# The attention norm's root moved from the query product's input to the attention scores

## What is computed

```python
def rms_norm(x, g):
    y = x * rsqrt(mean(x * x, axis=-1) + EPS)
    return y * g

x1 = x + merged @ w_out                       # end of the mixing layer

def cross_attention(x1, k, v, g, wq, wo):
    h = rms_norm(x1, g)
    q = (h @ wq).reshape(B, S, XA_HEADS, XA_HEAD_DIM)
    s = einsum('bshd,bmhd->bhsm', q, k) * (XA_HEAD_DIM ** -0.5)
    p = softmax(s, axis=-1)
    o = einsum('bhsm,bmhd->bshd', p, v)
    return o @ wo
```

## Time and profile before

| | us |
|---|---|
| median of 3 runs | 1138.18 |
| lowest, highest | 1137.84, 1140.97 |
| the profiled execution's own time | 1140.06 |
| its span in the trace | 1138.3 |

### The profile page before, as it was taken

How to read it: one execution, slowest core, us unless ns; L and a number is a source line. 1 busy time by engine, 2 the same in 40 slices (tenths; PEclk the granted TensorE clock), 3 DMA queues, 4 the chain that set the end, 5 groups by cost and what they waited for, 6 DMA issues and landing times.

```text
span 1138.3 us, 18382 instructions
## 1 busy us (share of the span) xinstructions
PE 1077.6 (95%) x5851; PEld 793.5 (70%) x5851; DVE 815.3 (72%) x1616; ACT 630.9 (55%) x932; POOL 231.7 (20%) x197
## 2 busy tenths in 40 slices
PE   6999999899799999999999999999999999999991
PEld 5998459899449977666666666666666666666660
DVE  4734724454862355579999999999999888999993
ACT  4384333233633351566666666666667665667663
POOL 1002220001000020232222233322223332323331
PEclk7999999999999999999999999999999999999996
DMA  9502415250826181899999999999999999999945
GB/s 304 208 1 81 150 77 223 83 219 16 340 104 233 64 346 48 231 320 361 354 368 366 370 364 369 365 357 359 367 371 363 364 358 362 365 365 357 349 133 168
DMA packets 63558, 301.70 MB, mean 265 GB/s; under 512 B 13175, under 2 KB 15843, under 8 KB 36886
## 3 DMA queue, kind: packets, MB, share of 16 engines
q1 hardware_dynamic: 47038, 261.93, 60.0%
q0 software_dynamic: 16480, 39.24, 14.5%
HBM read 282.65 MB, written 36.17 MB: 280 GB/s over the span
## 4 chain that ended last, share of the span: by engine, by line
PE 86%; DMA 6%; DVE 4%; ACT 2%; issue 1%; SPq 1%; DVEq 0%; POOLq 0%; ACTq 0%
PE pair L179 17%; PE pair L1950 15%; PE pair L1975 15%; PE pair L1941 10%; PE pair L1957 7%; PE pair L1717 5%; PE pair L1928 5%; PE pair L1621 3%; DMA regB<-in_exp_w_down 2%; PE pair L1833 2%; PE pair L1901 1%; DVE regL L1154 1%; DMA regB<-in_cache_mem_k 1%; PE pair L1964 1%; DMA regA<-in_w_in 1%; PE pS L1913 1%
## 5 line engine op out<-in xcount | busy, mean ns | idle before, releaser
L758 POOL DMA_INDIRECT acc_rows<-regL x64 | 123.3, 1926 | 423.0 <-DMA acc_rows<-regL 245.5
L1975 PE MATMUL pair<-hi_parts,act_parts 128*96 128x512 f32 x512 | 163.2, 400 | 1.2 <-DVE act_parts L1559 1.2
L179 PE MATMUL pair<-h_hi,w_parts 128*128 128x260 f32 x640 | 132.2, 288 | 3.7 <-DVE h_lo L1148 3.4
L1950 PE MATMUL pair<-hi_parts,x_parts 128*96 128x512 f32 x512 | 132.4, 401 | 0.0
L179 PEld LDWEIGHTS pair<-h_hi,w_parts 128*128 128x128 f32 x640 | 105.1, 192 | 4.8 <-issue 2.8
L1975 PEld LDWEIGHTS pair<-hi_parts,act_parts 128*96 128x96 f32 x512 | 79.6, 165 | 28.2 <-DVE act_parts L1559 1.3
L1950 PEld LDWEIGHTS pair<-hi_parts,x_parts 128*96 128x96 f32 x512 | 79.8, 165 | 27.8 <-issue 1.9
L742 POOL DMA_INDIRECT regL<-h_rows,regL x67 | 68.7, 1025 | 58.7 <-DVE regL L1405 28.9
L1555 DVE TENSOR_TENSOR regB_lo<-regB,hi_parts 128x2048 fp32r<-128x2048 f32 x32 | 73.1, 2284 | 10.4 <-ACT hi_parts L1062 10.4
L1555 DVE TENSOR_TENSOR regA_lo<-regA,hi_parts 128x2048 fp32r<-128x2048 f32 x32 | 73.1, 2285 | 9.3 <-ACT hi_parts L1062 9.1
L1565 DVE TENSOR_SCALAR regL<-pair,regL 96x512 f32<-96x512 f32 x64 | 47.7, 746 | 40.7 <-PE pair L1975 40.7
(11 more groups left out here) (357 smaller groups left out, 2350.0 us busy)
## 6 DMA issues: line engine op xcount, KB each, us to landing
regA<-in_exp_w_gate SPq DMA_DIRECT2D x32, 1024.0 KB, 9.5
regA<-in_exp_w_up SPq DMA_DIRECT2D x32, 1024.0 KB, 17.0
regA<-in_exp_w_down SPq DMA_DIRECT2D x32, 1024.0 KB
regB<-in_exp_w_down SPq DMA_DIRECT2D x32, 1024.0 KB, 19.3
regB<-in_exp_w_gate SPq DMA_DIRECT2D x16, 1024.0 KB, 9.4
regB<-in_exp_w_up SPq DMA_DIRECT2D x16, 1024.0 KB, 18.3
regC<-in_exp_w_gate SPq DMA_DIRECT2D x16, 1024.0 KB, 9.0
regC<-in_exp_w_up SPq DMA_DIRECT2D x16, 1024.0 KB, 19.7
```

The lines of the kernel that those rows point to most:

```text
L179: ins = pe.matmul(pair[p][:, h, 0:HALF], w, x[:, k, cols], start=k == 0 and i == 0, stop=k == KD - 1 and i == 2)
L758: pool.indirect_dma_start(acc_rows, bass.IndirectOffsetOnAxis(ap=sidx[0:SLOTS, r:r + 1].bitcast(U32), axis=0), yX[r][0:SLOTS, :], None, bo ...
L1950: pe.matmul(gu_out, x_parts[:, x, k, :], hi, start=False, stop=False, skip_group_check=True)
L1975: ins = pe.matmul(pair[2][0:SLOTS, h, :], act_parts[:, x, k, :], w[:, k, h * 512:(h + 1) * 512], start=k == 0 and s == 0, stop=k == KF - 1 ...
```

## The change

The norm is split. ACT now makes the query product's high part straight from x1 and the norm's weight (`x_hi2` = rounded `xT` x `g`), and DVE makes its low part in one operation (`xT` x `g` - `x_hi2`, into `h2_lo`); both are made slab by slab during x1. The spreading of `rs`, the norm's multiplication and the tile `htmp2` fall away. The token's number `rs` goes into the attention instead: the exponential's scale and the factor of the maximum are read from two small tables (`rs_scale`, `rs_minus`), and the sample tokens' queries are scaled as they are copied. The squares of all eight slabs are added by GpSimd, in a ring of three places, and summed in one round on TensorE, which stands behind the first two query slabs. The first three cuts of `wq` stand inside x1's last two slabs, with waits of their own (`room`) and a shifted ring (`shift`). Since the new high part lies where value cache 4 and 5 were loaded, these two loads (1 MB each) stand behind value cache 2 and 3.

```diff
     def cut_hi(self, a, u):
...
+        if u < len(self.room):
+            a.wait_ge(*self.room[u])
...
-    o += [(("x1", m), "dve") for m in range(KD)] + [("nb2", "dve")]
+    o += [(("x1", m), "dve") for m in range(KD)]
...
-        sqT, sqU = view(regL, 8392, KD, NT), view(regL, 13080, 3, NT)
+        sqT, sqU = view(regL, 8392, 3, NT), view(regL, 13080, 3, NT)
+        rs_scale, rs_minus = small[:, 24:29], small[:, 29:34]
...
-                         {0: wq_in}, w_parts, *split_q)
+                         {0: wq_in}, w_parts, *split_q, shift=2 * KD % SPLIT_RING,
+                         room=((made, J.no[("x1", KD - 2)] + 1), (split_o[2], KD), (made, J.no[("x1", KD - 1)] + 1)))
...
-            sp.wait_ge(ss_done, 3)
-            for i in (4, 5):
-                sp.dma_start(vc[i], cv[:, two(i), :]).then_inc(v_in[0], 16)
             sp.wait_ge(made, J.no[("q", KD - 1)] + 1)
...
             for i in (2, 3):
                 sp.dma_start(vc[i], cv[:, two(i), :]).then_inc(v_in[1], 16)
+            for i in (4, 5):
+                sp.dma_start(vc[i], cv[:, two(i), :]).then_inc(v_in[0], 16)
             sp.wait_ge(k_used, 2)
...
+            for m in range(1, KD):
+                pool.wait_ge(squares, 2 * KP + m + 1)
+                if m > 1:
+                    pool.wait_ge(x1_added, m - 1)
+                pool.tensor_tensor(sqT[:, 0, :], sqT[:, 0, :], sqT[:, sq_at(m), :], ALU.add).then_inc(x1_added, 1)
...
             for m in range(KD):
                 O.cut_hi(a, 2 * m + 3)
                 O.cut_hi(a, 2 * m + 4)
+                if m >= KD - 2:
+                    Q.cut_hi(a, m - (KD - 2))
                 J.wait_taken(a, ("x1", m))
-                squared(sqT[:, m, :], xT[:, m, :])
-            rooted(D)
+                cl = COL["norm_xattn"] + m
+                a.activation(x_hi2[:, m, :], xT[:, m, :], ACT.Copy, scale=par[:, cl:cl + 1]).then_inc(x_hi_made, 1)
+                if m == KD - 1:
+                    Q.cut_hi(a, 2)
+                if m > 2:
+                    a.wait_ge(x1_added, m - 2)
+                squared(sqT[:, sq_at(m), :], xT[:, m, :])
...
-            for u in range(2):
-                Q.cut_hi(a, u)
-            cut_norm(htmp2, 2 * KD)
-            Q.cut_hi(a, 2)
             for m in range(KD):
                 Q.cut_hi(a, 2 * m + 3)
                 Q.cut_hi(a, 2 * m + 4)
                 p = J.wait_made(a, ("q", m))
                 J.take(a.copy(halves(qT[:, m, :]), pair[p][:, :, 0:HALF]), ("q", m))
+                if m == 1:
+                    rooted(D)
+                if m == 2:
+                    a.wait_ge(inverse, c.n[id(root)])
...
-                                        scale=SCALE, accum_out=asum[:, r:r + 1]), ("s", *STEPS[n]))
+                                        scale=rs_scale[:, STEPS[n][1]:STEPS[n][1] + 1], accum_out=asum[:, r:r + 1]), ("s", *STEPS[n]))
...
+            def leave_x(m):
+                v.wait_ge(x_hi_made, m + 1)
+                cl = COL["norm_xattn"] + m
+                v.scalar_tensor_tensor(h2_lo[:, m, :], xT[:, m, :], par[:, cl:cl + 1], x_hi2[:, m, :].bitcast(F32),
+                                       ALU.mult, ALU.subtract).then_inc(x_lo_made, 1)
 
             residual("x1", 2 * KP)
-            inverted()
-            Q.cut_lo(v, 0)
-            Q.cut_lo(v, 1)
-            apply_split("nb2", xT, htmp2, h2_lo, "norm_xattn", 2 * KD)
+            leave_x(KD - 1)
             Q.cut_lo(v, 2)
...
             for u in range(3, Q.units):
                 Q.cut_lo(v, u)
+                if u == 7:
+                    inverted()
+                    v.wait_ge(inverse, c.n[id(inverse)])
+                    step(v.tensor_scalar(rs_scale, rs, SCALE, None, ALU.mult))
+                    step(v.tensor_scalar(rs_minus, rs, -SCALE, None, ALU.mult))
...
-                    c.add(v.tensor_scalar(nmax[:, r:r + 1], amax[:, r:r + 1], -SCALE, None, ALU.mult), att_max)
+                    t = STEPS[n][1]
+                    c.add(v.tensor_scalar(nmax[:, r:r + 1], amax[:, r:r + 1], rs_minus[:, t:t + 1], None, ALU.mult), att_max)
...
+            def query(n):
+                Q.product(pe, pair, n, x_hi2, h2_lo, (lambda k: pe.wait_ge(x_lo_made, k + 1)) if n == 0 else None)
 
             into_residual("x1", lambda m: O.product(pe, pair, m, h_hi, y_lo,
-                                                    (lambda k: pe.wait_ge(h_lo_made, KD + k + 1)) if m == 0 else None))
-            spread("nb2")
+                                                    (lambda k: pe.wait_ge(h_lo_made, KD + k + 1)) if m == 0 else None),
+                          meanwhile=lambda: (query(0), query(1)))
```

More of the change, by code:

```diff
@@ L135, with __init__ @@
 class SplitWeights:
-    def __init__(self, J, names, weights, arrived, parts, hi_made, lo_made, half_used):
+    def __init__(self, J, names, weights, arrived, parts, hi_made, lo_made, half_used, shift=0, room=()):
+        self.shift, self.room = shift, room
         self.J, self.names, self.weights, self.arrived, self.parts = J, names, weights, arrived, parts
@@ L155, in cut_hi, with slot @@
             a.wait_ge(self.half_used, old // 2 + 1)
-        a.copy(self.parts[:, u % SPLIT_RING, 0], self.weights(u // 2, u % 2)).then_inc(self.hi_made, 1)
+        a.copy(self.parts[:, self.slot(u), 0], self.weights(u // 2, u % 2)).then_inc(self.hi_made, 1)
+    def slot(self, u):
+        return (u + self.shift) % SPLIT_RING
     def cut_lo(self, v, u):
@@ L162, in cut_lo @@
         v.wait_ge(self.hi_made, u + 1)
-        v.tensor_tensor(self.parts[:, u % SPLIT_RING, 1], self.weights(u // 2, u % 2),
-                        self.parts[:, u % SPLIT_RING, 0].bitcast(F32), ALU.subtract).then_inc(self.lo_made, 1)
+        v.tensor_tensor(self.parts[:, self.slot(u), 1], self.weights(u // 2, u % 2),
+                        self.parts[:, self.slot(u), 0].bitcast(F32), ALU.subtract).then_inc(self.lo_made, 1)
     def product(self, pe, pair, n, acts_hi, acts_lo, ready=None):
@@ L174, in product @@
                     ready(k)
-                hi, lo = self.parts[:, u % SPLIT_RING, 0, j, :], self.parts[:, u % SPLIT_RING, 1, j, :]
+                hi, lo = self.parts[:, self.slot(u), 0, j, :], self.parts[:, self.slot(u), 1, j, :]
                 for h in range(2):
@@ L276, in trunk @@
             pass
+        with nc.sbuf_tensor("unused_L5", [P, 10240], F32), nc.sbuf_tensor("x_hi2", [P, KD, NT], F32R) as x_hi2:
+            pass
         regL = sb("regL", [P, 14640])
@@ L311, in trunk @@
         xsq = view(regL, 11432, D)
[L312 removed]
+        htmp1, ytmp, _ = view(regL, 11432, 2, NT), view(regL, 12552, 2, NT), None
         rawP, rawC, rawH = view(regL, 4232, DP), view(regL, 4232 + DP, DP), view(regL, 4232 + 2 * DP, DP)
@@ L452, in trunk @@
         s_exp = sem("s_exp")
+        x_hi_made, x_lo_made, x1_added = sem("x_hi_made"), sem("x_lo_made"), sem("x1_added")
         silu_done, gated, routed = sem("silu_done"), sem("gated"), sem("routed")
@@ L935, in sample_queries @@
                     a.wait_ge(q_stored, 16 * (h - 1))
-                J.take(a.copy(qsr[h % 2][0:DEC, :], bank[q][0:DEC, 0:HD]), ("qs", h))
-            for u in range(2):
-                Q.cut_hi(a, u)
-            cut_norm(htmp2, 2 * KD)
-            Q.cut_hi(a, 2)
+                J.take(a.activation(qsr[h % 2][0:DEC, :], bank[q][0:DEC, 0:HD], ACT.Copy, scale=rs[0:DEC, TT:NTT]), ("qs", h))
             for m in range(KD):
@@ L1778, in _ @@
             for n in range(KD):
-                Q.product(pe, pair, n, h_hi, h2_lo, (lambda k: pe.wait_ge(h_lo_made, 2 * KD + k + 1)) if n == 0 else None)
+                if n > 1:
+                    query(n)
                 if n >= 2 and n % 2 == 0:
```

22 lines of the change are left out of this document (13 added, 9 removed).

## The result

The changed kernel took 1128.14 us (median of 7 runs, 1125.19 to 1133.94); the kernel before took 1138.58 (7 runs, 1137.84 to 1140.97). The ratio is 0.991, with an interval of 0.989 to 0.9929. The profiled execution took 1128.14 itself, with a span of 1126.3, against 1140.06 and 1138.3 before.

A forecast was written before the change was run, and what follows sets the result against it. TensorE, holding 86% of the chain of waits, was taken to bound the kernel, with sums, root, norm and first slab in series. 1140.06 - 10.19 + 0.6 = 1130.5, less 1.88 gave 1128.6 us, range 1126.5 to 1133.0.

The forecast's parts named there:

- The sum of 10.19: From x1's end through the queries on TensorE: 10.19 us less in all.
- three terms: Gap before the first query slab, 7.28 us less; that slab, 4.21 less; one round of sums comes back, 1.30 more.
- The inputs in time: Low parts and weight cuts for the first query slabs are ready before TensorE wants them, covered by 2.5 us.
- T: The end of x1 on TensorE, at 220.42 us in the profile before, from which the prediction counts.
- the first rival: At x1's end: the first query slab still waits for its inputs, giving back up to 4.21 us: 1132.8; chance 14%.
- The stretching: DVE operations beside GpSimd's additions may lengthen, 0.70 to 1.56 us; three would be 2.6 us later, just within cover.
- the three operations whose cover was 2.5: DVE operations at x1's end feeding the query slabs; if stretched, 2.6 us later in all.
- The attention's 0.6: In the attention: the maximum's per-partition factor adds 0.6 us, half of 0.07 x 16; the exponential's scale adds 0.
- The loads at nothing: In the attention: value cache 4 and 5 queued later, 5 us more of DMA ahead of later loads, cost nothing.
- The slower rival: In x1: GpSimd's additions set the pace through ACT's squares; at 8 us per addition 1144.4; chance 3%.
- The last 1.88: Whole time: the median of the runs lies 1.88 us below the profiled execution, so 1130.5 becomes 1128.6.
- The gain carried to the end: Behind the attention: the rest is issued relative to what goes before, so all stages come about 10 us earlier.

The follow-up runs named there:

- the sums first: The changed kernel with the round of sums ahead of the first query slab in place of behind the second: 1134.76 us, ratio to before 0.9974.
- the round alone: The kernel before with all eight x1 squares added by GpSimd and one round of sums, norm unchanged: 1138.77 us, ratio 0.9997; again 1139.97 us, ratio 1.0002.

## Why the prediction was right

It said 1128.6 in a range of 1126.5 to 1133.0; the median was 1128.14. The mechanism is the one it gave. That the number came within 0.5 us is partly luck: the changed kernel's runs lie between 1125.19 and 1133.94, and the stage and the attention account for 9.70 (10.11 less 0.41) of the 10.44 between the two medians.

- **The sum of 10.19.** Measured 10.11. Its three terms hold one by one: no gap, two slabs in 11.50 (11.48 in the earlier trace rows), and 1.29 for the round (1.30). The kernel before is itself not fixed here: its stage was 58.23 and 58.79 in two executions, since more or less of its spreading runs at the lower clock level, 1.2 GHz (mean granted clock 1.00 and 0.67).
- **The inputs in time.** Low parts at T+2.5, as worked out. The third cut at T+3.1, predicted T+3.2. The last addition began at T+2.8 and left a cover of 7.3, predicted 7. The handovers between ACT and DVE cost no more than the rows had shown, so the first rival did not come.
- **The stretching.** It came, but in x1, one cut per slab, where VectorE still has 44% of its time free (18.2 of 41.78 us), and not in the three operations whose cover was 2.5. "DVE bore the cost and GpSimd did not grow" was read from one pair and is too narrow: with more additions GpSimd bore it too.
- **The attention's 0.6.** Measured 0.41, of which 0.31 or 0.32 is the root's price behind the wait for key cache 6 and the rest is when that load landed. The reason given, that the wait swallows delays ahead of it, is right: it swallowed 0.63 of 0.94, two thirds, where a half was taken. The factor's 0.06 per instruction is the per-read share taken. The exponential's price was put at 0 of a possible 0.1 and is 0.09: that term was mis-sized for the instruction. Sixteen of both are 2.4 us, and the root costs 0.94 in all, so most of this work lay beside the path.
- **The loads at nothing.** DVE's wait for key cache 6 was 1.15 and 1.49 us (1.69 in the earlier trace rows). `xa_wo` landed 15.4 us after its issue, 2.1 later than before and inside the bound of 5; nobody waited for it, nor for value cache 4 and 5, which landed near 302.
- **The slower rival.** With five times the additions' work the wait it rests on was there (1.05 and 3.46 us on ACT), and x1 did not move at all. What the prediction did not name is the other place where slow additions are paid, the round of sums behind the second slab.
- **The last 1.88.** It was taken off because the profiled execution lay above the median. From the attention's end on, the changed kernel's execution is 1.8 shorter, in stages that the change leaves alone (793.55 against 791.75), and the kernel before's own second execution shows 791.47 there. So of the 12.0 us between the two spans, 1.8 and the 0.5 by which x1 ended earlier are not the change's.
- **The gain carried to the end.** It was, here. So was the loss with the sums first (6.42 in the stage, 6.62 in the medians), but not that of the round alone (3.4 in the stage, 0.2 in the medians). That all behind is issued relative to what goes before is thus no proof by itself.

## What to carry to other kernels

Where a norm stands between two products that fill TensorE, its per-token number can be applied behind the product, if what follows up to there is linear in it, and then the sums only have to end somewhere later: put them behind as many slabs as their slowest input needs, because the place made more of the gain than all the rest, and one round by itself made none. Here the last addition ended 4.2 us behind x1, so one slab of 5.74 might have done; that was not run. A wait on TensorE can cost more than its length: in the stage, a round that goes (1.2 us) against a wait of 2.7 was a loss of about 3. When a load is late, look first at what stands ahead of it in its queue.

## What the runs showed of the hardware

- **After a short wait TensorE works slowly for a while.** After idle times of 2.69, 3.96 and 7.08 us the same ten matmuls took 2.00, 1.99 and 1.99 us in place of 1.16, at a granted clock of 0.50 (1.2 GHz) each time, and behind the second and the third the query slabs took 1.55 and 1.58 longer: nearly the same after 3.96 and after 7.08 us.
- **Two engines with SBUF operands take turns.** A GpSimd addition and a VectorE operation with two SBUF inputs that overlap end within 0.15 us of when they would if done one after the other, and the later one carries the time: VectorE 0.69 to 1.40, or GpSimd 1.31 to 1.78.
- **A number read per partition has a price for the instruction:** 0.06 us on a VectorE operation of one column, 0.09 on a ScalarE exponential of 256 columns that already read its bias so.
- **The rest of the program is not constant.** From the first expert product to the end the executions differ by 4.7 us (652.4 to 657.1) with the same program there, so a difference of 3 us in a stage can be plain in a trace and invisible in the whole.
